# A streaming encoder step in split fp32: x^T laid out by the host and normalised channel-major once, its split pair kept in a scratch tensor for the second pass, loops written out

## The reference

```python
h = rmsnorm(x, norm_g)             # x (L, 1024), over the channels
proj = h @ w_in                    # 1024 x 2832: attention, GLA and conv inputs and gates
y_attn = band_attention(q, k, v, sinks) * silu(ag)          # 512 columns
y_gla  = rmsnorm(gla_chunked(gq, gk, gv, log_a)) * silu(gg) # 256 columns
y_conv = (silu(layernorm(depthwise_conv(u))) @ w_pw + b_pw) * silu(cg)
y = concat([y_attn, y_gla, y_conv]) @ w_out
return x + y
```

## Time and profile before

| | |
|---|---|
| time, median of 3 runs | 1104.81 us (1102.08, 1104.81, 1105.5) |
| span of the profiled execution | 1102.7 us |
| TensorE busy | 1036.8 us, 94% |
| VectorE busy | 866.5 us, 79% |
| ScalarE busy | 560.7 us, 51% |
| GpSimd busy | 202.2 us, 18% |
| moved by DMA | 70.69 MB, mean 64 GB/s |

### The profile page before, as it was taken

The page is one execution under the profiler, slowest core; times in us unless marked ns, Lnnn a source line. Parts: engine busy times, 40 slices in busy tenths (PEclk is TensorE's granted clock), DMA queues, the critical chain, the costliest instruction groups (busy, mean ns, idle before and its releaser), DMA issues.

```text
span 1102.7 us, 18786 instructions
## 1 busy us (share of the span) xinstructions
PE 1036.8 (94%) x5818; PEld 867.9 (79%) x5818; DVE 866.5 (79%) x2629; ACT 560.7 (51%) x1317; POOL 202.2 (18%) x286
## 2 busy tenths in 40 slices
PE   4889999999999999986898999999999999999976
PEld 3768888888888888865676888888888888888854
DVE  6567777777777777767478899999999999999994
ACT  6565555555555555556554444344444433444431
POOL 0101111111111111000012332222323322323221
PEclk9999999999999999987898999999999999999988
DMA  8441111111111112203530111011111110111110
GB/s 288 148 45 59 58 58 58 57 57 57 57 57 57 57 48 76 81 32 103 158 134 1 58 58 40 30 46 57 57 57 57 57 57 22 45 38 38 40 32 30
DMA packets 53539, 70.69 MB, mean 64 GB/s; under 512 B 23695, under 2 KB 32092, under 8 KB 53500
## 3 DMA queue, kind: packets, MB, share of 16 engines
q1 hardware_dynamic: 53500, 70.22, 20.2%
HBM read 52.58 MB, written 17.69 MB: 64 GB/s over the span
## 4 chain that ended last, share of the span: by engine, by line
PE 86%; DVE 6%; ACT 3%; DMA 2%; issue 1%; POOL 1%; SPq 0%; DVEq 0%; ACTq 0%; POOLq 0%
PE J L475 46%; PE J L490 16%; PE S L1316 3%; PE S L1356 3%; PE T L1346 3%; PE T L448 2%; PE T L1491 2%; PE T L1458 1%; PE T L1288 1%; DVE acc L1250 1%; DMA wraw<-in_w_in 1%; PE S L1426 1%; PE S L1466 1%; PE S L1464 1%; ACT whi L367 1%
## 5 line engine op out<-in xcount | busy, mean ns | idle before, releaser
L475 PE MATMUL J<-whi,xhi 128*128 128x512 f32 (+2 forms) x816 | 302.9, 371 | 8.5 <-DVE xlo L459 4.5
L475 PE MATMUL J<-whi,xlo 128*128 128x512 f32 (+2 forms) x816 | 295.6, 362 | 0.0
L475 PE MATMUL J<-wlo,xhi 128*128 128x512 f32 (+2 forms) x816 | 295.5, 362 | 0.0
L1250 DVE SCALAR_TENSOR_TENSOR acc<-ub,convw,acc 128x128 f32<-128x128 f32 (+1 forms) x1020 | 283.3, 352 | 7.3 <-PE S L1466 7.3
L475 PEld LDWEIGHTS J<-whi,xhi 128*128 128x128 f32 x816 | 156.8, 192 | 31.9 <-DVE xlo L459 4.3
L475 PEld LDWEIGHTS J<-whi,xlo 128*128 128x128 f32 x816 | 155.4, 190 | 25.4
L475 PEld LDWEIGHTS J<-wlo,xhi 128*128 128x128 f32 x816 | 155.8, 191 | 21.7
L490 PE MATMUL J<-whi,yhi 128*128 128x512 f32 x272 | 114.6, 421 | 1.5 <-DVE ylo L1191 1.5
L490 PE MATMUL J<-wlo,yhi 128*128 128x512 f32 x272 | 108.2, 398 | 0.0
L490 PE MATMUL J<-whi,ylo 128*128 128x512 f32 x272 | 108.2, 398 | 0.0
L749 ACT ACTIVATE sc<-sc,nmx 128x256 f32<-128x256 f32 x136 | 68.1, 502 | 48.6 <-DVE nmx L948 48.6
(11 more groups left out here) (193 smaller groups left out, 1983.5 us busy)
## 6 DMA issues: line engine op xcount, KB each, us to landing
xin<-in_x_prompt SPq DMA_DIRECT2D x32, 512.0 KB, 3.6
out<-res SPq DMA_DIRECT2D x64, 256.0 KB, 2.0
res<-in_x_prompt SPq DMA_DIRECT2D x16, 512.0 KB, 4.2
res<-out SPq DMA_DIRECT2D x16, 512.0 KB, 4.3
wraw<-in_w_in SPq DMA_DIRECT2D x52, 128.0 KB, 2.6
wraw<-in_w_out SPq DMA_DIRECT2D x16, 256.0 KB, 3.5
wraw<-in_w_in SPq DMA_DIRECT2D x8, 256.0 KB, 4.2
res<-in_w_in SPq DMA_DIRECT2D x8, 256.0 KB, 5.1
```

What stands on the lines that cost most here:

```text
L475: last = nc.tensor.matmul(bank[:, 0:width], x[:, k, :], w, start=(k == 0 and n == 0), stop=(k == KT - 1 and n == 2))
L1250: nc.vector.scalar_tensor_tensor(acc[:, j, 0:frames], src, w, acc[:, j, 0:frames], ALU.mult, ALU.add).then_inc(conv_step, 1)
```

## The change

The host hands over x^T as well, laid out per tile as 128 channels x 8 groups x 128 frames. In pass A SP loads the frames once (`xtok`, for the sum of squares alone) and x^T (`xraw`). GpSimd spreads the inverse root over 128 columns (`rbc`), TensorE transposes that one block (`spread_rinv`), ScalarE copies it (`take_rinv`, `rb`), and GpSimd multiplies all of x^T by it (`norm_x`). ScalarE and VectorE then split 1024 columns in one instruction each, from SBUF. `xhi` and `xlo` have two buffers. SP stores both to a scratch tensor (`store_x`), and pass B only reads them back (`reload_x`): its square, scale, transposes and splits are gone. The constants of pass B are packed by the host into one array of 1.2 MB, loaded after pass A. All bodies run from t = -3, and the loops are written out.

The diff, cut to its core:

```diff
-        xin = [sb(f"xin{i}", [P, D]) for i in range(2)]
-        xn = sb("xn", [P, D])
-        xhi = sb("xhi", [P, KT, P], F32R)
-        xlo = sb("xlo", [P, KT, P], F32R)
+        xhi = [sb(f"xhi{i}", [P, KT, P], F32R) for i in range(2)]
+        xlo = [sb(f"xlo{i}", [P, KT, P], F32R) for i in range(2)]
...
-        def load_x(ps, t):
-            need(nc.sync, ps.xn_ready, t.n - 1)
+        def x_slot(ps, t):
+
+            return t.par if ps is A else 1 - t.par
+
+        def load_x(t):
+            need(nc.sync, x_squared, t.n)
             src, rows = x_rows(io["x_prompt"], io["x_sample"], t)
-            nc.sync.dma_start(xin[t.par][0:rows, :], src).then_inc(ps.x_loaded[t.par], 16)
+            nc.sync.dma_start(xtok[0:rows, :], src).then_inc(x_token, 16)
+            need(nc.sync, x_lo, t.n - 1)
+            src, rows = (xT_s[:, :, :], DEC) if t.n == LAST else (xT_p[t.n], P)
+            nc.sync.dma_start(xraw[t.par][:, :, 0:rows], src).then_inc(A.x_loaded[t.par], 16)
+
+        def store_x(t):
+            nc.sync.wait_ge(x_hi, t.n + 1)
+            nc.sync.dma_start(xs_hi[t.n], f(xhi[t.par][:, :, :])).then_inc(x_stored[t.par], 16)
+            nc.sync.wait_ge(x_lo, t.n + 1)
+            nc.sync.dma_start(xs_lo[t.n], f(xlo[t.par][:, :, :])).then_inc(x_stored[t.par], 16)
+
+        def reload_x(t):
+            slot = x_slot(B, t)
+            if t.n < 2:
+                nc.sync.wait_ge(A.projected[2], TILES - 1 + t.n)
+                for i in range(2):
+                    nc.sync.wait_ge(x_stored[i], 32 * ((TILES + 1 - i) // 2))
+            else:
+                nc.sync.wait_ge(B.projected[3], t.n - 1)
+            nc.sync.dma_start(f(xhi[slot][:, :, :]), xs_hi[t.n]).then_inc(B.x_loaded[slot], 16)
+            nc.sync.dma_start(f(xlo[slot][:, :, :]), xs_lo[t.n]).then_inc(B.x_loaded[slot], 16)
...
+            need(nc.gpsimd, rb_psum, t.n)
+            nc.gpsimd.tensor_tensor(rbc[:, :], rinv[:, :].to_broadcast([P, P]), root_b[:, :],
+                                    ALU.mult).then_inc(x_wide, 1)
+
+        def spread_rinv(t):
+
+            nc.tensor.wait_ge(x_wide, t.n + 1)
+            nc.tensor.transpose(T[1][:, 0:P], rbc[:, :], ident[:, :]).then_inc(rb_psum, 1)
+
+        def take_rinv(t):
+            nc.scalar.wait_ge(rb_psum, t.n + 1)
+            need(nc.scalar, x_normed, t.n)
+            nc.scalar.activation(rb[:, :], T[1][:, 0:P], ACT.Copy).then_inc(rb_taken, 1)
+
+        def norm_x(t):
+            nc.gpsimd.wait_ge(rb_taken, t.n + 1)
+            nc.gpsimd.wait_ge(A.x_loaded[t.par], 16 * (t.half + 1))
+            nc.gpsimd.tensor_tensor(xraw[t.par][:, :, :], xraw[t.par][:, :, :],
+                                    rb[:, :].unsqueeze(1).to_broadcast([P, KT, P]), ALU.mult).then_inc(x_normed, 1)
+
+        def split_x_hi(t):
+            nc.scalar.wait_ge(x_normed, t.n + 1)
+            need(nc.scalar, A.projected[2], t.n - 1)
+            if t.n >= 2:
+                nc.scalar.wait_ge(x_stored[t.par], 32 * t.half)
+            nc.scalar.activation(xhi[t.par][:, :, :], xraw[t.par][:, :, :], ACT.Copy).then_inc(x_hi, 1)
+
+        def split_x_lo(t):
+            nc.vector.wait_ge(x_hi, t.n + 1)
+            nc.vector.tensor_tensor(xlo[t.par][:, :, :], xraw[t.par][:, :, :], f(xhi[t.par][:, :, :]),
+                                    ALU.subtract).then_inc(x_lo, 1)
...
+            sp.dma_start(params[:, :], params_d).then_inc(consts_b, 16)
...
-                when(t + 2, lambda n: transpose_x(A, n, 0))
-                if t.fixed and t.n == LAST:
-                    transpose_x(B, B0, 0)
+                if t.n == -1:
+                    pe.wait_ge(rb_taken, 2)
+                when(t + 3, spread_rinv)
                 out(1)
...
-                if (t + 2).real() and not (t.fixed and t.n == -2):
-                    if t.real():
-                        need(pe, B.y_lo, t.n)
-                        pe.wait_ge(dec_ready, t.n + 1)
-                    transpose_x(B, t + 2, 0)
-                    transpose_x(B, t + 2, 1)
```

More of the change, by code:

```diff
@@ L427, in norm_scale @@
[L427 to L455, removed]
@@ L668, in body_b @@
                     ln_rinv(p)
-                if not (t.fixed and t.n == -2):
-                    when(t + 2, lambda n: norm_rinv(B, n))
                 if t.real():
@@ L703, in body_a @@
                     cache_hi(act)
-                if t1.real():
-                    split_x_hi(A, t1, 1)
-                if t.fixed and t.n == TILES:
-                    split_x_hi(B, B0, 1)
-                if t.fixed and t.n == -1:
+                if t.n < -1:
+                    when(t + 3, norm_square, take_rinv)
+                if t.n == -3:
+                    split_hi(A, 0, KT)
+                    split_x_hi(B0)
+                if t.n == -1:
                     split_hi(A, KT, 3 * KT)
@@ L736, in body_a @@
                     split_hi(B, 0, STAGES)
-                if not (t.fixed and t.n == -2):
-                    when(t + 2, lambda n: norm_square(A, n))
-                if t.fixed and t.n == LAST:
-                    nc.scalar.wait_ge(A.xT_psum, 2 * TILES)
-                    norm_square(B, B0)
+                if t.n >= -1:
+                    when(t + 3, norm_square)
                 if t1.real():
@@ L798, in body_a @@
                     pT_hi(3)
-                when(t + 2, lambda n: split_x_hi(A, n, 0))
-                if t.fixed and t.n == LAST:
-                    split_x_hi(B, B0, 0)
+                if t.n >= -1:
+                    when(t + 2, split_x_hi)
+                    when(t + 3, take_rinv)
                 if t.real():
@@ L848, in body_b @@
                     nc.scalar.activation(ez[:, :], ez[:, :], ACT.Ln, bias=1.0).then_inc(z_ln, 1)
-                if not (t.fixed and t.n == -2):
-                    when(t + 2, lambda n: norm_square(B, n))
                 if t.real():
@@ L866, in body_b @@
                     nc.scalar.activation(enb[:, :], S[1][:, 0:P], ACT.Exp, scale=-1.0).then_inc(cum_exp, 1)
-                if not (t.fixed and t.n == -2):
-                    when(t + 2, lambda n: norm_scale_act(B, n))
                 if p.real():
@@ L906, in body_b @@
                                          scale=0.5).then_inc(th_ready, 1)
-                if not (t.fixed and t.n == -2):
-                    when(t + 2, lambda n: split_x_hi(B, n, 0), lambda n: split_x_hi(B, n, 1))
                 if t1.real():
@@ L1077, in body_a @@
                     y_half(0)
[L1078 to L1080 removed]
+                if t.n >= -1:
+                    when(t + 2, split_x_lo)
                 if t.fixed and t.n == TILES:
@@ L1232, in body_b @@
                                                    ALU.mult, ALU.mult).then_inc(go_n, 1)
-                if not (t.fixed and t.n == -2):
-                    when(t + 2, lambda n: split_x_lo(B, n, 0), lambda n: split_x_lo(B, n, 1))
                 if p.real():
```

226 lines of the change are left out of this document (106 added, 120 removed).

## The result

The changed kernel takes 1138.72 us (median of four runs, 1136.97 to 1140.35) against 1104.15 for the kernel before in the same comparison (four runs, 1102.08 to 1105.5): a ratio of 1.031, interval 1.029 to 1.033. It is slower; 1142 was forecast. The traces compare by span: 1135.4 us against 1102.7, 32.7 more. (The note on the kernel before takes time and span of one execution as the same. They are not: wherever both are on record the time is 1.6 to 1.9 us longer, 1136.97 against 1135.4 here. That is most of the 2.1 us which the prediction adds to its sum. The medians differ by more than the spans, 34.6 us, as the profiled execution is the fastest of its four.) One execution of the kernel before, beside runs 5 and 8, was in a slower state (1177.6 us) and is left out.

The account below looks back on a forecast made before the run. TensorE, busy for 94% of the span, was taken as the bound. Terms: 1102.7 + 5 + 34.2 + 0.5 + 14 - 13.0 - 2.5 = 1140.9 us, put at 1142 for the median; range 1096 to 1156.

Parts of the forecast that it names:

- start of pass A, first tile's extra included: Pass A's first projection comes later: weight splits behind `take_rinv` and GpSimd's multiply, more x^T to load; +5 us, bounds +2 and +9.
- hold and chain: Pass A, tiles 0 to 13: GpSimd's multiply holds VectorE's L1045, delaying split, addition and TensorE; 2.44 us each, +34.2.
- last two tiles: Body 14 of pass A, where only the undisturbed stall is left: +0.5 us.
- clock: TensorE's granted clock falls after gaps in pass A: 1.3 us in 11 of 14 tiles, +14 us, bounds 0 and 22.
- turn: Between the passes: a normalisation and an `xlo` wait go, constants delay w_out pieces; net -2.5 us, bounds -5 and +4.
- pass B, 15 bodies: All eight transposes leave TensorE in pass B, -0.88 us per tile: -13.0 us, bounds -13.5 and -8.
- The undisturbed part: Pass A without the hold: longer split, then addition, stall TensorE by 1.3 us against a saving of 0.76.
- No slack at that projection: Next tile's first projection in pass A: whatever delays VectorE's addition L500 delays TensorE; addition ends 235.36, TensorE starts 235.47.
- The written-out loops: Loops of both passes written out: 0 us, +5 if code loading is felt.
- Rival 1: GpSimd holds nothing up in pass A: stall 1.3 us, no clock loss; 1097.8 us, about 1100 as median; chance 0.17.
- Rival 3: x is ready in time and both passes gain what the transposes promise: 1078.6 us; chance 0.05.

Follow-up runs that it names:

- run 5: Changed kernel with GpSimd's multiply only after VectorE's low half of the x split, and TensorE's first projection waiting for one addition less: 1098.5 us, 0.993.
- run 8: Kernel before with three useless multiplies of 864 columns on VectorE ahead of its x split in each tile of pass A: 1169.9 us, 1.058.
- run 1: Changed kernel with one more wait: GpSimd's multiply of x^T starts only after VectorE's low half of the x split: 1106.8 us, 1.0022.
- run 4: Changed kernel with pass A's x split moved forward and TensorE's first projection waiting for one addition less: 1091.2 us, 0.988.
- run 7: Kernel before with one useless GpSimd multiply of 128x864 in each tile of pass A, its result read by nobody: 1131.6 us, 1.026.
- run 6: Changed kernel with GpSimd's multiply of x^T cut into two of 512 columns, one behind the other: 1139.8 us, 1.033.
- run 10: Changed kernel with early x split, projection waiting for one addition less, and at the start tile 1's scales copied later, w_out pieces loaded earlier: 1081.0 us, 0.980.
- run 9: Kernel before with its loops written out and nothing else changed: 1104.8 us, 1.0011.

## Why the prediction was right

The mechanism was the one forecast, and runs 1, 4 and 7 show it from three sides. The total was closer than its parts: the sum said +38.2 us, the spans differ by 32.7, and some terms were off by more and in both directions. That they cancelled so far is luck.

| term | forecast | in the trace |
|---|---|---|
| start of pass A, first tile's extra included | +5 | +7.7 to the first scores, +4.8 in the first period |
| hold and chain | +34.2 (14 tiles, 2.44 each) | +28.9 (13 tiles, 2.22 each) |
| last two tiles | +0.5 | +0.7 |
| clock | +14 (1.3 in 11 tiles) | about +8.8 (1.46 in 6 tiles) |
| turn | -2.5 | -5.4 |
| pass B, 15 bodies | -13.0 | -14.0, of it -1.7 in the first body |
| end | 0 | +1.2 |
| sum | +38.2 | +32.7 |

The 28.9 is 13 x (30.00 - 27.78); the clock is 6 x 1.46; the first period is 33.98 against 29.13; the turn is the time from pass A's last scores to pass B's first cumulative sum, 64.46 us against 69.91.

- *The hold.* GpSimd's multiply: 2.4 us forecast, 2.37. L1031 "over 2 us": 2.20. Split 1.15, measured 1.21. The hold stands in body 0 too, but TensorE waited only 0.96 us there, for the x split, since that projection needs no addition; so it is paid in 13 tiles and not in 14. The stall was 2.98 instead of 3.2 (30.00 - 27.78 + 0.76; 2.66 of it is the wait before the projection), mainly because GpSimd led VectorE by 0.45 us where I had 0.3 and so held it shorter. By the rule of the page "SBUF — State Buffer" of the Trainium skill (section "SBUF: two separate sides"), the lock lasts a whole instruction; run 6 agrees: 1.12 us, then 2.28, one hold per half.
- *The undisturbed part.* I gave the chain without the hold a stall of 1.3 us and a net +0.54 per tile. Run 1 has 28.22, which is +0.44. The split in SBUF, one instruction of 1024 columns ahead of the addition, is thus a cost of its own, without any hold. It and the longer start are why run 1 only draws level with the kernel before, though pass B gained its 14 us.
- *No slack at that projection.* Shown by run 7 (1.56 us in, 1.57 out).
- *The clock.* Right in kind, too large in size: 14 us against 8.8. I took a low clock in 11 of 14 tiles at 1.3 us, and it was 6 of 13 at 1.46.
- *The start* was mis-sized: 12.5 us with all of tile 0, where I had 5 and 2.4 of the hold's. Some of it is the clock's: in the first period the mean granted clock was 0.90, and 0.94 before, which is up to 1.7 us (the same estimate as in run 10). I had priced `take_rinv` ahead of tile 0's splits, and not the second `take_rinv` ahead of the next weights (3.65 us). And I named SP's queue only in the turn: at the start the load of tile 3 waits there for tile 1's split with the w_out pieces behind it (3.73 us of ScalarE). Run 10 takes 2.3 and 5.4 us back, the latter in part through the clock.
- *The turn.* The gain was 3 us more. The windows of both:

```profile
493.21:563.12 69.91, 52.91 (x229) 43.56 (x230) 46.28 (x114) 43.32 (x90) 5.16 (x13) 0.80 0.49 141
...
544.07:608.53 64.46, 48.09 (x214) 38.95 (x214) 43.52 (x109) 37.32 (x79) 4.12 (x6) 0.87 0.59 182
```

  The mean clock is 0.80 before and 0.87 after, by the same estimate worth up to 5.6 us, so the clock can account for the surplus, and I had no clock in this term. Nor is the length steady: run 9, with the instructions of the kernel before, has 67.78 us at 0.85. In the chain of TensorE's waits there, that for the probabilities went from 6.2 to 5.0 us, those at pass B's first projections from 2.3, 0.8 and 3.8 to one of 4.8, and one behind ScalarE's `glrT` grew from 1.4 to 3.7. I didn't take these apart by a run, so whether my estimates of the chain of weight splits and of the constants were right stays open.
- *The written-out loops*: 0, as forecast, by run 9.

Rival 1 (about 1100 without a hold) was some 7 us too low: run 1 is that case, 1106.8. Its span of 1101.7 is 3.9 over my 1097.8, with 8.7 us at the start (8.1 to the first scores, 0.6 in the first period) where I had 3. Rival 3, both passes gaining, had a span of 1078.6. The order written in this change can't reach it, but run 10 with the same design has 1079.0 (and a time of 1081.0).

## What to carry to other kernels

Before an element-wise step is given to GpSimd, look in VectorE's timeline for what runs beside it: in these traces a GpSimd instruction with two operands in SBUF held VectorE's own steps with two operands in SBUF to its end (2.20 us instead of 0.43), and the price was paid only where another engine waited for those. So place it, and any longer split, where no wait of the bounding engine ends; here the same instructions in another order, with one wait relaxed, are worth 58 us (1138.7 to 1081.0). And where a stall brings down TensorE's clock, a step that shortens the stall can show no gain by itself (2.66 to 2.16 us: none), and a larger one can gain more than its own length (to 0.9 us: 32 us in all), so try such steps together as well as singly.

## What was unexpected of the hardware

- The clock loss doesn't grow simply with the wait. Waits of 2.66 us lost it in every second tile (period 30.00 or 31.45), waits of 2.16 us in 11 of 13 (31.0 or 29.46), and 2.67 us without the multiply on GpSimd (run 8) in none of the first four steady tiles and then in eight of ten. Waits of 0.9 and 1.1 us (runs 1 and 7) lost none. What decides between two tiles of the same wait stays open.
- The hold seems to work the other way too, and over more than one instruction. In pass B of the changed kernel GpSimd's L681 of 128x256 averages 3132 ns, where its twin L675 had 1913 before and the shortest of either took 0.73 us. It starts in the middle of an unbroken row of VectorE's convolution steps and ends 0.6 us after the row does (733.19 against 732.59); in the kernel before L675 does the same (660.75 against 660.15), only its start lies later in the row. That it waits for a gap is how I read it, and no run tested it.

```profile
729.70 3.49 POOL L681 TENSOR_TENSOR thg<-thg,braw 128x256 f32<-128x256 f32 x1 [2.22 <-ACT thg L856]
728.83 3.76 DVE L1233 SCALAR_TENSOR_TENSOR acc<-ub,params,acc 128x128 f32<-128x128 f32 x14
...
L681 POOL TENSOR_TENSOR thg<-thg,braw 128x256 f32<-128x256 f32 x17 | 53.2, 3132 | 59.1 <-ACT thg L856 59.1
```
